# One expert slot in four is added into the residual tile by VectorE instead of through TensorE and a diagonal matrix

## What is computed

```python
def peer_ffn(h, w_query, subkeys, u_table, v_table):
    ...
    def one_block(xb):                       # 128 tokens
        ...
        experts = ...                        # (128 tokens, 128 slots)
        gates = jax.nn.softmax(top_s, axis=-1).reshape(PEER_BLOCK, PEER_HEADS * PEER_TOPK)
        u = u_table[experts]
        hid = jax.nn.gelu(jnp.einsum('nkd,nd->nk', u, xb).astype(jnp.float32), approximate=False) * gates
        return jnp.einsum('nk,nkd->nd', hid.astype(xb.dtype), v_table[experts])
    ...
h = h + peer_ffn(rmsnorm(h, ffn_norm_w[l]), ...)
```

## Time and profile before

| | |
|---|---|
| time, median of three runs | 3041.13 us (3040.42 to 3041.49) |
| span of the profiled execution | 3041.8 us |
| first gather to the end of slot 511 | 521.7 to 1943.8 us |
| DMA in 521 to 1945 us | busy share 1.00, 411 GB/s |
| PE, DVE, ACT, POOL busy in that stretch | 1238, 1035, 734, 592 of 1424 us |
| TensorE's granted clock in that stretch | 0.98 |

### The profile page before, as it was taken

The page is one execution under the profiler, slowest core; times in us unless marked ns, Lnnn a source line. Parts: engine busy times, 40 slices in busy tenths (PEclk is TensorE's granted clock), DMA queues, the critical chain, the costliest instruction groups (busy, mean ns, idle before and its releaser), DMA issues. The chain is left out here.

```text
span 3041.8 us, 32500 instructions
## 1 busy us (share of the span) xinstructions
PE 2669.7 (88%) x11426; PEld 1824.8 (60%) x11426; DVE 1897.9 (62%) x3880; ACT 1286.3 (42%) x2790; POOL 673.9 (22%) x638
## 2 busy tenths in 40 slices
PE   6998777998889877789999999699798698999998
PEld 6975647344444322245555555499686456788887
DVE  5866836767777677777777776555564655343323
ACT  2224313544444454555556555444234245232222
POOL 3320000434443443444444344100000020000000
PEclk9996788999999999999999999899898698999999
DMA  6860024999999999999999999666231001323332
GB/s 219 309 205 1 1 92 138 416 414 395 421 420 421 400 414 420 417 411 419 419 412 416 404 418 413 245 188 193 71 94 27 37 22 42 104 70 97 97 98 76
DMA packets 131732, 750.81 MB, mean 247 GB/s; under 512 B 17409, under 2 KB 17937, under 8 KB 65249
## 3 DMA queue, kind: packets, MB, share of 16 engines
q0 software_dynamic: 81824, 575.43, 46.6%
q1 hardware_dynamic: 49744, 173.30, 16.7%
HBM read 746.57 MB, written 2.10 MB: 246 GB/s over the span
## 5 line engine op out<-in xcount | busy, mean ns | idle before, releaser
L1533 PE MATMUL peer_y<-rows,diag 128*128 128x512 f32 x2048 | 997.0, 614 | 177.5 <-ACT diag L1513 165.9
L1487 DVE CUSTOM_DVE_ANT_0 rows<-rows,hidden 128x1024 f32<-128x1024 f32 x512 | 627.8, 1226 | 373.6 <-DMA rows<-in_peer_table,experts 370.5
L1474 POOL DMA_INDIRECT rows<-in_peer_table,experts x512 | 592.5, 1157 | 1035.9 <-PE peer_y L1533 794.5
L1533 PEld LDWEIGHTS peer_y<-rows,diag 128*128 128x128 f32 x2048 | 364.1, 192 | 592.8 <-ACT diag L1513 298.0
L1510 ACT ACTIVATE hid<-hid 128x1 f32<-128x1 f32 x512 | 102.6, 200 | 542.1 <-DVE hid L1487 535.8
L2136 DVE TENSOR_TENSOR piece_w_low<-piece_raw,piece_w_high 128x1024 fp32r<-128x1024 f32 x132 | 161.1, 1223 | 102.3 <-ACT piece_w_high L2131 102.2
L1513 ACT ACTIVATE diag<-ident,hid 128x128 f32<-128x128 f32 x512 | 205.6, 402 | 16.7
L2131 ACT ACTIVATE piece_w_high<-piece_raw 128x1024 fp32r<-128x1024 f32 x132 | 138.5, 1052 | 107.8 <-PE out_bank L152 77.6
L417 ACT ACTIVATE proj_w_high<-proj_raw 128x1024 fp32r<-128x1024 f32 (+2 forms) x57 | 57.7, 1014 | 237.9 <-PE proj_bank L152 237.8
L1511 ACT ACTIVATE hid<-hid,gates 128x1 f32<-128x1 f32 x512 | 150.8, 295 | 16.6
L150 PE MATMUL peer_y<-peer_feat_high,early_w_high 128*128 128x256 f32 x352 | 143.6, 408 | 1.2 <-issue 1.2
(11 more groups left out here) (525 smaller groups left out, 5663.6 us busy)
## 6 DMA issues: line engine op xcount, KB each, us to landing
ada<-in_w_ada POOLq DMA_DIRECT2D x96, 384.0 KB, 4.8
piece_raw<-in_ffn_w_gate SPq DMA_DIRECT2D x44, 512.0 KB, 3.6
piece_raw<-in_ffn_w_up SPq DMA_DIRECT2D x44, 512.0 KB, 4.5
piece_raw<-in_ffn_w_down SPq DMA_DIRECT2D x44, 512.0 KB, 3.6
query_raw<-in_peer_w_query SPq DMA_DIRECT2D x32, 512.0 KB
early_raw<-in_ffn_w_gate SPq DMA_DIRECT2D x22, 512.0 KB
early_raw<-in_ffn_w_up SPq DMA_DIRECT2D x22, 512.0 KB
early_raw<-in_ffn_w_down SPq DMA_DIRECT2D x22, 512.0 KB
```

The source lines that it names most:

```text
L1474: pool.indirect_dma_start(self.rows[:, b, :], None, self.table, bass.IndirectOffsetOnAxis(ap=self.experts[:, unit % self.SETS, n % TOPK:n ...
L1487: dve.tensor_tensor_reduce(out=self.rows[:, b, 0:D], in0=self.rows[:, b, 0:D], in1=self.hidden[:, tile, :], scale=1.0, scalar=0.0, op0=ALU ...
L1533: last = pe.matmul(self.y[self.bank(tile)][:, c * BANK:(c + 1) * BANK], self.diag[:, b, :], self.rows[:, b, D + c * BANK:D + (c + 1) * BAN ...
```

## The change

Slots with n % 4 = 1 (128 of 512) take another way. ACT stops after the weight and makes no diagonal matrix for them; PE skips them; and DVE multiplies the slot's v by the weight and adds it straight into the residual tile with one instruction over 128x1024 elements (`vector_sum`). That instruction stands behind the dot of slot n + 2 and waits for ACT's weight. It frees the buffer through a counter of its own, `vector_free`. The waits on the old counters are renumbered, since these now count three slots in four.

```diff
@@ gathers
-            if n >= self.RING:
-                pool.wait_ge(self.slot_free, n - self.RING + 1)
+            if n >= self.RING and self.by_vector(n - self.RING):
+                pool.wait_ge(self.vector_free, self.vector_slots(n - self.RING + 1))
+            elif n >= self.RING:
+                pool.wait_ge(self.slot_free, n - self.RING + 1 - self.vector_slots(n - self.RING + 1))
@@ dots
                                      accum_out=self.hid[:, 0, b:b + 1]).then_inc(self.dotted, 1)
+            if n >= 2 and self.by_vector(n - 2):
+                self.vector_sum(dve, n - 2)
             self.route(dve, 1)
...
+    def vector_sum(self, dve, n):
+        b, x = n % self.RING, self.t.x[:, n // SLOTS, :]
+        before = self.vector_slots(n)
+        dve.wait_ge(self.weight_ready, before + 1)
+        if before:
+            dve.wait_ge(self.vector_free, before)
+        dve.scalar_tensor_tensor(x, self.rows[:, b, D:2 * D], self.hid[:, 2, b:b + 1], x, ALU.mult, ALU.add)\
+           .then_inc(self.vector_free, 1)
+
     def add(self, dve, tile):
         x = self.t.x[:, tile, :]
-        dve.wait_ge(self.slot_free, (tile + 1) * SLOTS)
+        all_of = self.vector_slots((tile + 1) * SLOTS)
+        dve.wait_ge(self.slot_free, (tile + 1) * SLOTS - all_of)
+        dve.wait_ge(self.vector_free, all_of)
@@ weights
-            chain.link(act.activation(self.hid[:, 2, b:b + 1], self.hid[:, 1, b:b + 1], ACT.Copy,
-                                      scale=self.gates[:, unit % self.SETS, n % TOPK:n % TOPK + 1]))
-            act.activation(self.diag[:, b, :], self.t.ident[:, :], ACT.Copy, scale=self.hid[:, 2, b:b + 1])\
-               .then_inc(self.diag_ready, 1)
+            weight = act.activation(self.hid[:, 2, b:b + 1], self.hid[:, 1, b:b + 1], ACT.Copy,
+                                    scale=self.gates[:, unit % self.SETS, n % TOPK:n % TOPK + 1])
+            if self.by_vector(n):
+                weight.then_inc(self.weight_ready, 1)
+            else:
+                chain.link(weight)
+                act.activation(self.diag[:, b, :], self.t.ident[:, :], ACT.Copy, scale=self.hid[:, 2, b:b + 1])\
+                   .then_inc(self.diag_ready, 1)
@@ sums
-            pe.wait_ge(self.diag_ready, n + 1)
+            if self.by_vector(n):
+                self.n_pe += 1
+                continue
+            pe.wait_ge(self.diag_ready, n + 1 - self.vector_slots(n + 1))
```

More of the change, by code:

```diff
@@ L1419 @@
     LOGIT_SLOT = 11
+    EACH = 4
     def __init__(self, core, ctx, t, hidden, scores, room):
@@ L1449, in __init__ @@
             core.sem(f"route_{n}") for n in ("routed", "logits", "exped", "gated")]
-        self.dotted, self.diag_ready, self.slot_free, self.added = [
-            core.sem(f"slot_{n}") for n in ("dotted", "diag_ready", "free", "added")]
+        self.dotted, self.diag_ready, self.weight_ready, self.slot_free, self.vector_free, self.added = [
+            core.sem(f"slot_{n}") for n in ("dotted", "diag_ready", "weight_ready", "free", "vector_free", "added")]
         self.routing = self.routes()
@@ L1455, in advance, with by_vector, vector_slots @@
         self.start += k
+    def by_vector(self, n):
+        return n % self.EACH == 1
+    def vector_slots(self, n):
+        return sum(self.by_vector(i) for i in range(n))
     def bank(self, tile):
@@ L1623, in route_unit @@
         if unit >= SETS:
-            self.dve.wait_ge(self.diag_ready, (unit - SETS + 1) * TOPK)
+            used = (unit - SETS + 1) * TOPK
+            self.dve.wait_ge(self.diag_ready, used - self.vector_slots(used))
         self.dve.tensor_scalar(self.gates[:, unit % SETS, :], soft[:, 1, :], soft[:, 2, 1:2], None, ALU.mult)\
```

## The result

| | before | after |
|---|---|---|
| median of the runs, us | 3041.31 (3040.42 to 3042.23) | 3072.07 (3064.71 to 3073.32) |
| span of the profiled execution, us | 3041.8 | 3069.3 |
| mean granted clock | 0.942 | 0.925 |

The ratio is 1.0093, with a 95% interval of 1.0081 to 1.0106: the change costs 31 us where 4 were forecast, and 8 more than the upper end of the range allowed.

The account below looks back on a forecast made before the run. The prediction took the DMA transfer of 512 MB of rows and the weights beside them as the bound. Its terms, -2 + 0 + 2 + 3 + 1 = +4 us on 3041.13, gave 3045 us, range 3036 to 3064.

Parts of the forecast that it names:

- The bound: In the slots, 521 to 1945 us, DMA transfer of rows and weights binds; the change moves only whether the queue stays filled.
- PE's share, -2 us: 128 slots fewer on PE, up to 253 us, lie beside full DMA; gain 2 us, bounds 0 and 10.
- The rival of a hidden PE limit: PE limits the slots where DMA rates fell short; filling those four pieces gives 3031 us; chance of faster 0.08.
- DVE's new instruction, +2 us: 164 us more on DVE, covered by dots' idle time except where cover is thin; cost 2 us, bounds 0 and 5.
- The buffer comes free later, +3 us: Every fourth buffer's gather is issued 3.1 us later, nearly covered by the queue; cost 3 us, bounds 0 and 26.
- The loop: Dot, new instruction, handover and empty lag: 8.7 to 9.6 us for four slots, against 9.95 us of transfers; fits, barely.
- those two gathers: Gathers of slots 178 and 179, taken as meeting a dry queue; their lags of 6.9 and 6.0 us served as empty lag.
- The rival (a), the loop binds: Dot, new instruction, issue and transfer set the slots' pace; 0.1 us more per slot gives 3055, 0.2 gives 3067; chance 0.26.
- What would show it: Signs in the slots: forecast, DMA share 1.00, lags near 7 us behind vector slots; loop, lags 6 to 7, share under 0.99.
- The rival (b), TensorE's clock: PE idles at skipped slots, its clock falls and sums come late at some heads; 3061 us; chance 0.12.
- The rival (c), held gathers: POOL's gathers in the slots are held while DVE's new instruction runs; 29 us, 3060 if half showed; chance 0.04.
- The tail, +1 us: At the last two slots PE restarts slowly after idling 3.0 us; cost 1 us, bounds 0 and 2.

Follow-up runs that it names:

- e4: The changed kernel without DVE's new instructions, every fourth slot's v part left out; POOL waits for ACT's weight instead: 3041.93 us, ratio 0.9994.
- e2: The kernel before plus a DVE instruction of the same form at the same places, which nobody waits for: 3044.03 us, ratio 1.0006.
- e9: e4 with the buffer released when ACT has made the diagonal of slot n + 2, almost the changed kernel's time: 3067.59 us, ratio 1.0074.
- e3: e2 with POOL also waiting for the added instruction ahead of the gather: 3103.24 us, ratio 1.0190.
- e5: e4 with the buffer released at the end of the dot of slot n + 2: 3041.36 us, ratio 0.9998.
- e1: The changed kernel with the new instruction behind the dot of slot n + 1 instead of n + 2: 3045.79 us, ratio 1.0015.
- e7: The kernel before with five buffers for the rows in place of six: 3096.76 us, ratio 1.0190.

## Why the prediction was wrong

- **The bound: right.** DMA transfers set the pace and all that mattered was whether the queue stayed filled. e4 takes a quarter of PE's sums away and gains nothing that can be told.
- **PE's share, -2 us: right.** PE became 185 us lighter, not up to 253, and e4 bounds the gain by 5 us (0.9985). The rival of a hidden PE limit is out.
- **DVE's new instruction, +2 us: right.** 163.9 us against the 164 worked out, and e2 puts the cost of such work at -1 to +5 us where no buffer waits for it. The wait for ACT's weight cost nothing: 0.0 us idle ahead of L1514.
- **The buffer comes free later, +3 us: the step that failed.** It measured some 23 us by e9; from the first gather to the last dot the changed kernel lost 29. My upper bound was 26. The loop was the right frame, and the number of slots in it too, and 9.95 us for four undisturbed slots is the measured median; two of the loop's terms were too small. *The handover*, taken as 0.1, is 0.27, and it stood in the rows of before: PE ends slot 505 at 1928.95 and the gather starts at 1929.23. *The lag*, taken as 6.0 to 6.9 from two gathers that met a dry queue, is 8.1 to 8.2 in the loop. So the loop is 10.9 us where I wrote 8.7 to 9.6, against 10.39 for four slots of the stretch before. "The loop fits, barely" turned into 0.5 us too long on average in each cycle of the stretch.
- **Why those two gathers were the wrong rows.** Fewer were ahead of them. When the gather of slot 179 started at 1002.56, two dots before its own were still to come: that of 178 at 1006.16 and that of 177 at 1002.89. So its 6.0 us were no empty lag either. The one that counts joins a queue in which three are still on their way: at 1249.53 the dots of slots 264, 265 and 266 were still to come. In the cycle above, the transfer ahead was over by 1254.13, and 2.49 us more would have been 1256.6; the dot started at 1257.64. I took the lag as the larger of two limits, the empty lag and the queue's work. Near the place where they are equal it was more than either, by 1 us here.
- **The rival (a), the loop binds, is what happened**, at 0.26. Its price of 12 us for each 0.1 us was high: e3 lost 31 us for some 0.6 us more, 5 us for each 0.1. With its point of decision placed by too short a lag, it looked like a matter of single late dots.
- **What would show it: half right.** POOL's longest waits ended by the new instruction, as said for the loop. I had asked for lags of 6 to 7 us and a DMA share under 0.99 too; they read 8.1 us and 0.99. By my signs a lag of 8.1 us was healthier than the 7 of the forecast, and it went with the loss.
- **The rival (b), TensorE's clock: it fell, at no cost.** 0.98 to 0.94 over the slots, and 0.93 in e4 and e5, which lose nothing. e3, where it reads 0.97 over the slots, loses twice as much as the change. The Trainium skill, TensorE: Matmul & The Clock Gate, HAM oscillation, says that waits between bursts of matmuls send the clock down again and again. The trace agrees that it falls (0.94), and e4 shows that it costs nothing beside a full DMA queue here.
- **The rival (c), held gathers: no.** A gather took 1182 ns on average instead of 1157, 13 us in all, on an engine that waits for 835 between its gathers. In e1 it is 1211, and that kernel loses a sixth as much.
- **The tail, +1 us: not what happened.** The slow restart did not come. PE idled 2.0 us ahead of slot 510 and its four matmuls took 1.98 us, as before; the last line is slot 511:

```profile
1965.59 1.98 PE L1564 MATMUL peer_y<-rows,diag 128*128 128x512 f32 x4 [2.01 <-ACT diag L1541]
1968.06 1.98 PE L1564 MATMUL peer_y<-rows,diag 128*128 128x512 f32 x4 [0.48 <-ACT diag L1541]
```

From the last dot to the end of that sum are 4.27 us, before 4.26. The 1.3 us more up to the end of the kernel are within what single executions differ by: e1, with the same tail, has 1101.1 us there, 1 less than before, and e4 1105.3.

No version here beats the kernel before. e1 is the form in which the change can be had nearly for nothing.

## What to carry to other kernels

Put a buffer's way round as a loop (release, handover, lag until the data is used) and compare it with the time that the queue needs for as many transfers; take the lag from gathers that have as many others ahead of them. With a lag of 8.15 us the loop of e5 comes to 9.6 us and was free, that of the changed kernel comes to 10.9 and was not, with 10.4 us for the four transfers. A slack of half a microsecond, reckoned with the lag of two single gathers, decides nothing. When work moves to an engine with idle time, ask first when its buffer comes free, since 156 us of such work alone were free here (e2) and a release 3.3 us later cost 1%. Put the releasing instruction as early as its inputs allow, and leave room between two late ones.

## What the runs showed of the hardware

- The DMA share hides a short queue. In 1040 to 1320 us e9's 393 GB/s and the 415 of e5 stand beside shares of 0.99 and 1.01, since a packet of 8 KB itself takes longer, 0.329 us on average against 0.317. The long packets are those of the late gathers: with the trace's packets taken in order, 128 to a gather, they took 0.347 us in e9 (slots 196 to 296), the others 0.313 to 0.327, and in e5 all lie at 0.315 to 0.321. Why they are slow, no run here explains.
- A gather with two semaphore waits ahead of it started 0.77 us behind the event that released it (e3), one with a single wait 0.27 us (the changed kernel). That the second wait is the reason is argued, not shown.
- Three slots on their way do not carry the full rate: with a lag of 8.4 us and a period of 2.74 (e7) there are, by this estimate, 3.1 at a time, against 4.0 in the kernel before (10.5 / 2.60), and 394 GB/s are moved between 1040 and 1320 us in place of 417.
